# First head's gate behind its scores, one remainder for the keys, and a final norm shared with GpSimd, in a hybrid retention and neighbourhood attention backbone

## The reference

```python
def _rmsnorm(x, w):
    y = x * lax.rsqrt(jnp.mean(x * x, axis=-1, keepdims=True) + NORM_EPS)
    return y * w
# retention, one head, block by block:
inner = einsum(einsum(q, k) * dmat, v)          # scores, decayed, times values
out = (silu(g) * o * rsqrt(mean(o * o))) @ w_out
# neighbourhood attention, one head:
s = (q * scale) @ k.T + bias                    # local window and context
p = softmax(s); y = (p @ v) @ w_out
# the end
return _rmsnorm(x, final_norm_w)
```

## Time and profile before

| | us |
|---|---|
| median of 3 runs | 2062.96 (2062.32 to 2063.7) |
| profiled execution | 2064.2 |
| its span | 2062.2 |
| PE busy | 1982.4 (96%) |
| DVE busy | 1331.9 (65%) |
| ACT busy | 755.3 (37%) |
| POOL busy | 97.1 (5%) |
| mean granted TensorE clock | 0.987 of full |

### The profile page before, as it was taken

One profiled execution on the slowest core, in us unless ns is written; L12 is line 12 of the kernel. 1 busy time (PEld: TensorE's weight loads), 2 busy tenths in 40 slices (PEclk: granted clock), 3 DMA queues, 4 the chain that ended last, 5 costly groups with the idle time before them and its releaser, 6 DMA issues.

```text
span 2062.2 us, 30027 instructions
## 1 busy us (share of the span) xinstructions
PE 1982.4 (96%) x10560; PEld 1699.1 (82%) x10560; DVE 1331.9 (65%) x2238; ACT 755.3 (37%) x1281; POOL 97.1 (5%) x162
## 2 busy tenths in 40 slices
PE   5999999999999989999999999799999889999997
PEld 5878888888888878888888888688888778788886
DVE  7866635735635677766664667777777667557375
ACT  5424223223313444312321233556556445333232
POOL 0000000000000000000000000311111000000000
PEclk9999999999999999999999999999999989999998
DMA  7221311321221122243324324211111223223222
GB/s 293 84 91 62 110 65 53 102 72 62 82 92 62 54 70 92 92 133 102 99 99 136 99 97 153 100 47 42 56 46 36 92 72 102 92 93 100 92 94 100
DMA packets 51257, 186.41 MB, mean 90 GB/s; under 512 B 5680, under 2 KB 5680, under 8 KB 51184
## 3 DMA queue, kind: packets, MB, share of 16 engines
q1 hardware_dynamic: 37744, 136.73, 19.9%
q0 software_dynamic: 13440, 48.63, 7.2%
HBM read 181.15 MB, written 4.19 MB: 90 GB/s over the span
## 4 chain that ended last, share of the span: by engine, by line
PE 83%; DVE 9%; issue 4%; ACT 2%; DMA 1%; DVEq 0%; SPq 0%; ACTq 0%; POOLq 0%
PE acc L393 58%; PE o_ps L497 3%; PE o_ps L532 3%; PE acc L620 3%; PE acc L497 2%; PE o_ps L663 2%; PE acc L678 2%; PE acc L519 2%; PE acc L462 2%; PE o_ps L678 1%; DVE pt_lo L1648 1%; PE acc L653 1%; PE acc L713 1%; PE o_ps L434 1%; DVE w_lo L1185 1%
## 5 line engine op out<-in xcount | busy, mean ns | idle before, releaser
L818 ACT ACTIVATE w_hi<-raw 128x1024 fp32r<-128x1024 f32 x232 | 245.1, 1057 | 595.8 <-PE acc L393 476.5
L1185 DVE TENSOR_TENSOR w_lo<-raw,w_hi 128x1024 fp32r<-128x1024 f32 x232 | 284.2, 1225 | 272.6 <-ACT w_hi L818 271.0
L393 PE MATMUL acc<-h_hi,w_hi 128*128 128x512 f32 x1520 | 434.7, 349 | 4.8 <-DVE w_lo L1185 3.4
L393 PE MATMUL acc<-h_hi,w_lo 128*128 128x512 f32 x1520 | 436.6, 350 | 0.0
L393 PE MATMUL acc<-h_lo,w_hi 128*128 128x512 f32 x1520 | 433.6, 348 | 0.0
L393 PEld LDWEIGHTS acc<-h_hi,w_hi 128*128 128x128 f32 x1520 | 245.4, 188 | 46.1 <-ACT u L1004 4.2
L393 PEld LDWEIGHTS acc<-h_hi,w_lo 128*128 128x128 f32 x1520 | 244.2, 188 | 37.7
L393 PEld LDWEIGHTS acc<-h_lo,w_hi 128*128 128x128 f32 x1520 | 243.2, 188 | 38.9
L1348 DVE SCALAR_TENSOR_TENSOR x<-acc,mod,x 128x512 f32<-128x512 f32 (+3 forms) x136 | 81.9, 637 | 144.9 <-PE acc L393 134.1
L393 PE MATMUL acc<-act_hi,w_lo 128*128 128x512 f32 (+1 forms) x396 | 120.1, 357 | 0.0
L393 PE MATMUL acc<-act_lo,w_hi 128*128 128x512 f32 (+1 forms) x396 | 119.4, 355 | 0.0
(11 more groups left out here) (234 smaller groups left out, 3524.2 us busy)
## 6 DMA issues: line engine op xcount, KB each, us to landing
raw<-in_weights_dram SPq DMA_DIRECT2D x232, 512.0 KB, 3.3
ada_raw<-in_ada_dram POOLq DMA_DIRECT2D x80, 512.0 KB, 3.6
ada_start<-in_ada_first_dram SPq DMA_DIRECT2D x8, 1024.0 KB, 18.3
x<-in_x_in_dram SPq DMA_DIRECT2D x4, 768.0 KB, 7.1
park_dram<-x POOLq DMA_DIRECT2D x1, 2048.0 KB, 8.1
rel<-in_bias_dram POOLq DMA_DIRECT2D x16, 128.0 KB, 2.3
x<-park_dram POOLq DMA_DIRECT2D x2, 1024.0 KB, 6.5
out_dram<-x SPq DMA_DIRECT2D x8, 256.0 KB, 2.2
```

Source lines behind the costliest of these rows:

```text
L393: mm = nc.tensor.matmul(tile[:, c0:c0 + cn], wt[:, b * P:(b + 1) * P], mv[:, n, c0:c0 + cn], start=(n == 0 and m == 0), stop=(n == last an ...
L818: nc.scalar.activation(w_hi[i][:, :], raw[i][:, :], ACT.Copy).then_inc(hi_split, 1)
L1185: nc.vector.tensor_tensor(w_lo[i][:, :], raw[i][:, :], w_hi[i][:, :].bitcast(F32), ALU.subtract)\
```

## The change

First head: on ScalarE `gate(0)` moves behind the rounding of scores 0 and 1 (its wait for the rotated keys goes), and on VectorE the chunk's `split()` moves behind decays 0 and 1 and their remainders. Keys: `nk_lo` has 64 partitions; its remainder is made once for each head, and its product takes only the rounded queries (rows 0 to 63 of `nq`), so that the term remainder of queries times remainder of keys is left out. Roots: four of them (after the retention's output, both FFNs and the attention's output) get their table load earlier, ahead of the wait for the last output tile. Final norm: ScalarE scales tiles 0 and 1 by the norm weight before the root; TensorE spreads the root a second time, into another bank; ScalarE copies that into SBUF; GpSimd multiplies tiles 0 and 1 by it; VectorE makes tiles 2 to 7. SP sends in the order 2, 3, 0, 4, 5, 1, 6, 7.

```diff
@@ -206,7 +206,7 @@
             rel = [sb(f"rel{i}", [P, 256], stack=stage) for i in range(2)]
             nq = sb("nq", [P, 2, LAT], F32R, stage)
             nk_hi = sb("nk_hi", [P, 2, TOK], F32R, stage)
-            nk_lo = sb("nk_lo", [P, 2, TOK], F32R, stage)
+            nk_lo = sb("nk_lo", [ND, 2, TOK], F32R, stage)
             nv_hi = sb("nv_hi", [P, TT, 2, P], F32R, stage)
             nv_lo = sb("nv_lo", [P, TT, 2, P], F32R, stage)
             prob = [sb(f"prob{a}", [P, TILES[a][1] * P + CTX], stack=stage) for a in range(QB)]
@@ -254,6 +254,7 @@
         npv_done, no_taken = sem("npv_done"), sem("no_taken")
         q_full, q_taken, out_used = sem("q_full"), sem("q_taken"), sem("out_used")
         x_ready, x_out = sem("x_ready"), sem("x_out")
+        x_scaled, pool_ready = sem("x_scaled"), sem("pool_ready")
@@ -293,8 +294,11 @@
                     sp.wait_ge(lo_split, i * 2 + (slot - 1))
                     sp.dma_start(raw[slot][:, :], weights[bass.ds(i * 2 + slot, 1), :, :].rearrange("a p n -> p (a n)"))\
                       .then_inc(raw_in[slot], 16)
-            for k in range(KC):
-                sp.wait_ge(x_ready, k + 1)
+            for k in (2, 3, 0, 4, 5, 1, 6, 7):
+                if k < 2:
+                    sp.wait_ge(pool_ready, k + 1)
+                else:
+                    sp.wait_ge(x_ready, k - 1)
                 sp.dma_start(out[:, k, :], x[:, k, 0:LAT]).then_inc(x_out, 16)
             sp.wait_ge(x_out, 16 * KC)
@@ -353,6 +357,10 @@
             pool.wait_ge(parked, 16)
             pool.dma_start(x[:, 0:4, 0:LAT], park[:, 0:4, :]).then_inc(x_back[0], 16)
             pool.dma_start(x[:, 4:KC, 0:LAT], park[:, 4:KC, :]).then_inc(x_back[1], 16)
+            pool.wait_ge(spread_copied, 2)
+            pool.wait_ge(x_scaled, 2)
+            for k in range(2):
+                nc.gpsimd.tensor_tensor(x[:, k, 0:LAT], x[:, k, 0:LAT], ss[:, 0:LAT], ALU.mult).then_inc(pool_ready, 1)
         @block.tensor
@@ -639,10 +647,11 @@
                 pe.wait_ge(s_taken, s_left.now() + max(i, 1))
                 tile = o_ps[:, 1 + i % 2, :]
                 q = nq[:, hh, a * P:(a + 1) * P]
+                q_hi = nq[0:ND, hh, a * P:(a + 1) * P]
                 w0, wn = WIN[a][0] * ROWS, WIN[a][1] * ROWS
                 for c0, k0, n in ((0, w0, wn), (wn, LAT, CTX)):
-                    for m, nk in enumerate((nk_hi, nk_lo)):
-                        mm = nc.tensor.matmul(tile[:, c0:c0 + n], q, nk[:, hh, k0:k0 + n], start=(m == 0), stop=(m == 1))
+                    for m, (qs, nk) in enumerate(((q, nk_hi), (q_hi, nk_lo))):
+                        mm = nc.tensor.matmul(tile[:, c0:c0 + n], qs, nk[:, hh, k0:k0 + n], start=(m == 0), stop=(m == 1))
                 mm.then_inc(s_full, 1)
             def turn_probs(i):
@@ -798,6 +807,10 @@
             ffn(LATENT)
             final_sums(LAT)
             spread_roots(LATENT)
+            for t in range(LAT // P):
+                mm = nc.tensor.matmul(o_ps[:, 1, t * P:(t + 1) * P], rms[:, t:t + 1].to_broadcast([P, P]), ident,
+                                      start=True, stop=True)
+            mm.then_inc(spread_done, 1)
         @block.scalar
@@ -837,8 +850,12 @@
                     nc.scalar.activation(S[k % 2][:, 0:width], src[:, k, 0:width], ACT.Square).then_inc(sq_done, 1)
                 squares_added.up(n)
-            def root(n, width):
+            def load_root():
                 nc.scalar.activation(nothing[:, :], ones[:, 0:1], ACT.Sqrt)
+
+            def root(n, width, loaded=False):
+                if not loaded:
+                    load_root()
                 act.wait_ge(sums_done, roots.up())
                 t = width // P
                 nc.scalar.activation(rms[:, 0:t], sums[:, 0:2 * t].rearrange("p (t c) -> p t c", c=2)[:, :, 0],
@@ -880,7 +897,7 @@
             def norm(layer, shift, parts):
                 width = TOK if len(parts) > 1 else LAT
-                root(D, width)
+                root(D, width, True)
                 for k in range(KC):
                     act.wait_ge(norm_t, normed.up())
                     for c0, cn, c in parts:
@@ -955,11 +972,13 @@
                     nc.scalar.activation(p_hi[i % 2][:, :], S[i % 2][:, 0:LAT], ACT.Copy).then_inc(p_hi_done, 1)
                 if first:
-                    act.wait_ge(qk_lo_done, 4)
-                    gate(0, *wait_at(0))
+                    _, gate_full, _, _ = A.next_at(0)
                 decayed(0)
                 decayed(1)
-                if not first:
+                if first:
+                    act.wait_ge(acc_full, gate_full)
+                    gate(0, 0, acc[0])
+                else:
                     split()
                     gate(0, *wait_at(0))
                 for i in range(2, 7):
@@ -1025,6 +1044,8 @@
                                 final_square(t, after, 2 * i + 2, m, width)
                     if last:
                         for m in range(2):
+                            if m:
+                                load_root()
                             t, after = wait_after()
                             if not ends:
                                 split()
@@ -1048,6 +1069,8 @@
                 head_attention(False)
             for c in range(OUT_SLOTS):
                 for m in range(2):
+                    if c == OUT_SLOTS - 1 and m:
+                        load_root()
                     t, after = wait_after()
                     if m:
                         split()
@@ -1153,6 +1176,8 @@
             for m in range(KC):
                 t = 1 if m in (0, 1, 2, 5, 7) else 0
                 _, full, _, after = A.next_at(t)
+                if m == KC - 1:
+                    load_root()
                 act.wait_ge(acc_full, full)
                 if m >= 3:
                     split()
@@ -1160,7 +1185,12 @@
             x_final()
             norm(1, 24, PARTS[:1])
             ffn(1, PARTS[:1], True)
-            root(D, LAT)
+            for k in range(2):
+                nc.scalar.activation(x[:, k, 0:LAT], x[:, k, 0:LAT], ACT.Identity, scale=norm_w[:, 4, k:k + 1])\
+                  .then_inc(x_scaled, 1)
+            root(D, LAT, True)
+            act.wait_ge(spread_done, roots.now() + 1)
+            nc.scalar.activation(ss[:, 0:LAT], o_ps[:, 1, :], ACT.Copy).then_inc(spread_copied, 1)
         @block.vector
@@ -1455,7 +1485,6 @@
                 if first:
                     A.next_at(0)
-                    split()
                     decay(0)
                     decay(1)
                 else:
@@ -1470,8 +1499,8 @@
                         made.then_inc(v_lo_done, 1)
                 decayed_lo(0)
                 decayed_lo(1)
+                split()
                 if not first:
-                    split()
                     A.next_at(0)
                     split()
                 for i in range(2, 7):
@@ -1653,10 +1682,8 @@
                 if hh == 0:
                     dve.wait_ge(acc_full, full)
                 dve.wait_ge(n_hi_done, n_hi_made.up(2))
-                for half in range(2):
-                    own = slice(half * ND, (half + 1) * ND)
-                    ins = nc.vector.tensor_tensor(nk_lo[own, hh, :], acc[t][hh * ND:(hh + 1) * ND, 0:TOK],
-                                                  nk_hi[own, hh, :].bitcast(F32), ALU.subtract)
+                ins = nc.vector.tensor_tensor(nk_lo[:, hh, :], acc[t][hh * ND:(hh + 1) * ND, 0:TOK],
+                                              nk_hi[0:ND, hh, :].bitcast(F32), ALU.subtract)
                 if hh == 1:
                     ins.then_inc(acc_taken[t], 1)
                     split()
@@ -1755,7 +1782,7 @@
             own_done()
             one_over(LAT)
             rooted()
-            for k in range(KC):
+            for k in range(2, KC):
                 nc.vector.scalar_tensor_tensor(x[:, k, 0:LAT], x[:, k, 0:LAT], norm_w[:, 4, k:k + 1], spread[:, 0:LAT],
                                                ALU.mult, ALU.mult).then_inc(x_ready, 1)
```

## The result

The changed kernel takes 2101.91 us (median of 4 runs, 2100.69 to 2105.04), the kernel before 2063.33 (4 runs, 2062.32 to 2064.21): ratio 1.0189, 95% interval 1.0175 to 1.0204. It is 1.9% slower; the forecast was 2058.3 with a range that ended at 2062.2. The profiled execution took 2101.68, its span is 2099.9, 37.7 longer than before.

A forecast was written before the change was run, and what follows sets the result against it. TensorE, with 83% of the chain, was taken to bound the kernel. The terms -5.1 - 1.3 + 0 + 1.7 = -4.7 us, from a median of 2062.96, gave 2058.3, range 2056.8 to 2062.2.

The forecast's parts named there:

- I cost its 64 rows at nothing: Keys' remainder product in the attention scores: its 64 rows cost 0; bounds 0 and 0.16 us for each change of shape.
- The rival: Score products: entering a 64-row product costs one product's overlap, 128 x 0.16 = 20.5 us, giving 2078.8; chance 0.13.
- First head: Before the first head's value products: wait falls from 3.8 to 1.54 us, full clock stays; -5.1 (bounds -2.2 and -5.3).
- The falling clock as a rival: First head: TensorE's clock falls all the same after a wait of 1.54 us; total -1.8, 2061.1; chance 0.19.
- Keys' remainder on VectorE: Boundaries between pairs: VectorE comes 1 us earlier, each gives 0.19, at 7 boundaries -1.3 us (bounds 0 and -1.8).
- Root table: Four roots with the table load moved earlier: 0; at the last root a gain of 0.15 us at most.
- Final norm: Tail: output transfers stand still after tiles 2 and 3 until GpSimd's tile 0; +1.7 us (bounds +1.1 and +2.7).

## Why the prediction was wrong, point by point

**The step that failed** is "I cost its 64 rows at nothing". Its bounds were right: a full product not overlapped, 0.28 - 0.12 = 0.16 for each change of shape, and the runs show 0.15 to 0.16. I chose the lower bound, 0, with the argument that weight loads of 128 columns hide fully behind products; that was a row of products of one shape, and said nothing of a change. The upper bound for 256 changes is 41 us, and with it the forecast would have been 2099.3, against 2101.9 measured. The rival named the mechanism, but counted it once for each remainder product ("entering costs one product's overlap", 20.5 us, 2078.8); the trace shows the same price on the way back, so even the rival was half of it. It had a chance of 0.13 and lay outside the range.

The Trainium skill, page TensorEngine Tiling, section Tiling Modes (Key Properties), says that a change of the tiling mode drains TensorE. The trace agrees, if a product over 64 of the 128 rows counts as such a mode, with 0.16 us for each change, either way. The Trainium skill, page TensorE: Matmul & The Clock Gate, section Step-by-step: what each phase is for, says that a weight load's time goes by columns and not by rows; that agrees too (0.18 for 64 rows, 0.19 for 128), and is why the duration of the load told nothing: what is lost is its cover.

**First head: the mechanism right, the exact size in part luck.** The wait was forecast at 1.54 and read at 1.5, and the clock stayed. The forecast of -5.1 and the -5.1 read later go back to the same trace of before, where the half clock cost 1.2 us more than in five of the six other traces that have this place unchanged. Against those the edit gives 3.9. The runs say 4.7 (2.7 to 6.8), which holds both. The falling clock as a rival is out: none of the traces of kernels with this edit has a clock under 1.00 there. Nothing of what was moved behind the scores came late.

**Keys' remainder on VectorE: the place right, the size too small.** Forecast 0.19 for a boundary. The six turning products free the array after 0.57 and not 0.66 (five starts of 0.11 lie between, not six), so it is 0.24 to 0.29, seven times, and within the last pair another 0.6. By the shifts -2.9 and not -1.3.

**Root table: 0 as forecast for the runs.** I had not seen that at the last root it keeps PE's clock up (with the earlier root 0.3 to 1.0 us from the sums to the end, by which unchanged trace it is held against), nor that the shared norm needs it.

**Final norm: wrong by its own steps, and the sum looked better than it was.** The pause of the transfers came as described (a share of 0.33 from 2090 to 2091), GpSimd's product took 1.24 (1.30 forecast), but the two spreads ended 3.7 behind the start of the sums (2084.20 to 2087.88) and not 5.6, because the root came 0.27 earlier and PE kept its full clock. By the transfers alone the tail would have been 0.3 shorter than before: SP's end comes 11.3 behind the start of the sums (2084.20 to 2095.5), and 11.6 before (2050.44 to 2062.0). Then GpSimd's drain puts 4.2 on top. Term: +1.7 forecast, +4.0 in the trace, by a step that I didn't have at all: the closing instructions of each engine belong to the tail, and GpSimd's was in the trace of before, 11.97 us long, where it cost nothing.

**Sum.** -5.1 at the first head, +38.1 in the pairs, +4.0 in the tail. What else the shifts show, +0.4, +1.8 and -1.5, is not the change's: around 720 to 740 the traces of the ten kernels, each against the same trace of before, move by -0.1 to +1.9, and the larger moves are there with and without any edit near it (PE's granted clock over 22 us there is 0.77 before and 0.69 after). Near 2018 the kernel before had 0.62 behind the wait at L620, and the changed kernel 1.00 behind the same wait of 1.9. Why one execution keeps its clock there and another doesn't stays open; it bounds what one trace can tell to some 2 us.

## What to carry to other kernels

Here a product over 64 rows among products over 128 saved nothing in columns and broke the overlap of weight loads on both sides: pad with zeros to the shape of its neighbours, or put products of one shape side by side. When an operation's cost isn't in the trace and the bounds lie 40 us apart over all its repetitions, the count of repetitions decides how far the range must reach, and the count must be of every transition, there and back. And before an engine gets work near the end, read its closing drain in the trace: an estimate from these rows is that GpSimd's last instruction costs nothing if it ends some 9 us before the end of the span (8.2 to its DRAIN's end, 0.6 from there to the span's). And hold a gain of a microsecond or two against several traces of the unchanged kernel: the first head's 5.1 was 3.9 against most of them.

## What the runs showed of the hardware

- A change between a product over 64 rows and one over 128 costs TensorE 0.15 to 0.16 us, in either direction: the weight load behind it starts only with its own product. Two 64-row products side by side overlap.
- Behind GpSimd's last instruction of this program its closing drain takes another 8.2 to 8.3 us (a product of 512 columns: 8.3; a memset of one column: 8.2). In the kernel before, where its last instruction issued a transfer, the DRAIN ended 10.9 behind it. What it does in that time no row says.
- The granted clock behind a wait of 1.9 us was 0.62 in one execution and 1.00 in another. Behind the same wait of 3.8 us the twelve value products of the first head took 5.26 us in two traces and 4.35 to 4.42 in five.
